# Splitting the queries and keys of an attention step into high and low fp32r parts, scores as three passes

## What is computed

```python
qa = rms_norm(heads(qa, N_HEADS_A), g_qa)      # 8 heads of 64, the same for ka, qb, kb
...
def forget_attend(q, k, v, Fq, Fk, qpos, kpos):
    logits = jnp.einsum('bthd,bshd->bhts', q, k).astype(jnp.float32) * (HEAD_DIM ** -0.5)
    logits = logits + (jnp.transpose(Fq, (0, 2, 1))[:, :, :, None] - jnp.transpose(Fk, (0, 2, 1))[:, :, None, :])
    logits = jnp.where((kpos[None, :] <= qpos[:, None])[None, None], logits, MASK_VALUE)
    p = jax.nn.softmax(logits, axis=-1).astype(v.dtype)
    return jnp.einsum('bhts,bshd->bthd', p, v)
```

## Time and profile before

| | us |
|---|---|
| median of three runs | 978.58 (977.5 to 979.12) |
| the profiled execution | 978.89 |
| its span | 977.1 |
| TensorE busy | 940.6 (96% of the span) |
| VectorE busy | 489.6 (50%) |
| ScalarE busy | 393.0 (40%) |
| GpSimd busy | 139.6 (14%) |
| mean granted TensorE clock | 0.982 of full |

### The profile page before, as it was taken

How to read it: one execution, slowest core, us unless ns; L and a number is a source line. 1 busy time by engine, 2 the same in 40 slices (tenths; PEclk the granted TensorE clock), 3 DMA queues, 4 the chain that set the end, 5 groups by cost and what they waited for, 6 DMA issues and landing times.

```text
span 977.1 us, 19815 instructions
## 1 busy us (share of the span) xinstructions
PE 940.6 (96%) x7546; PEld 861.4 (88%) x7546; DVE 489.6 (50%) x1154; ACT 393.0 (40%) x813; POOL 139.6 (14%) x139
## 2 busy tenths in 40 slices
PE   8889989899999989999999998999999999999998
PEld 7588668778788878998899998999999999999997
DVE  2553767864635686841157547454333244542232
ACT  3254655654566766433223224433211134431221
POOL 4100232141234575300000000000000000000000
PEclk9789999999999999999899999999999999999999
DMA  9536673354423564777323330323322333223212
GB/s 317 199 104 181 183 256 115 114 163 128 140 71 92 170 211 144 237 218 238 107 65 91 105 87 23 109 86 94 100 86 86 90 101 89 86 87 104 89 44 88
DMA packets 176233, 124.54 MB, mean 127 GB/s; under 512 B 14739, under 2 KB 152019, under 8 KB 176164
## 3 DMA queue, kind: packets, MB, share of 16 engines
q1 hardware_dynamic: 176034, 123.50, 41.5%
q10 hardware_dynamic: 130, 0.10, 0.0%
HBM read 116.99 MB, written 6.59 MB: 126 GB/s over the span
## 4 chain that ended last, share of the span: by engine, by line
PE 71%; issue 19%; DVE 7%; ACT 2%; POOL 1%; POOLq 0%; ACTq 0%; DVEq 0%
PE bank L952 19%; PE bank L953 18%; PE bank L954 18%; PE bank L1033 2%; PE bank L1056 2%; PE bank L1012 2%; PE bank L1042 2%; PE bank L859 1%; PE bank L1074 1%; PE bank L881 1%; PE bank L1087 1%; PE bank L1018 1%; PE bank L1097 1%; DVE sel L1881 1%; DVE ms L1926 0%
## 5 line engine op out<-in xcount | busy, mean ns | idle before, releaser
L952 PE MATMUL bank<-h_hi,w_hi 128*128 128x260 f32 x1360 | 397.3, 292 | 9.8 <-DVE h_lo L1765 6.5
L953 PE MATMUL bank<-h_lo,w_hi 128*128 128x260 f32 x1360 | 388.1, 285 | 0.0
L954 PE MATMUL bank<-h_hi,w_lo 128*128 128x260 f32 x1360 | 387.7, 285 | 0.0
L952 PEld LDWEIGHTS bank<-h_hi,w_hi 128*128 128x128 f32 x1360 | 259.8, 191 | 32.5 <-issue 24.4
L953 PEld LDWEIGHTS bank<-h_lo,w_hi 128*128 128x128 f32 x1360 | 260.1, 191 | 0.0
L954 PEld LDWEIGHTS bank<-h_hi,w_lo 128*128 128x128 f32 x1360 | 259.9, 191 | 0.0
L952 PE MATMUL bank<-u_hi,w_hi 128*128 128x260 f32 x512 | 145.2, 284 | 0.0
L953 PE MATMUL bank<-u_lo,w_hi 128*128 128x260 f32 x512 | 144.8, 283 | 0.0
L954 PE MATMUL bank<-u_hi,w_lo 128*128 128x260 f32 x512 | 144.8, 283 | 0.0
L2222 DVE TENSOR_TENSOR w_lo<-raw,w_hi 128x1024 fp32r<-128x1024 f32 x62 | 76.0, 1226 | 135.1 <-ACT w_hi L1641 135.1
L1641 ACT ACTIVATE w_hi<-raw 128x1024 fp32r<-128x1024 f32 x62 | 65.4, 1055 | 140.3 <-PE bank L954 140.3
(11 more groups left out here) (316 smaller groups left out, 1178.1 us busy)
## 6 DMA issues: line engine op xcount, KB each, us to landing
raw<-in_w_in SPq DMA_DIRECT2D x44, 512.0 KB, 4.1
part<-in_w_ada SPq DMA_DIRECT2D x32, 512.0 KB, 5.6
raw<-in_w_up SPq DMA_DIRECT2D x32, 512.0 KB, 4.1
raw<-in_w_down SPq DMA_DIRECT2D x32, 512.0 KB, 4.1
ada<-in_w_ada SPq DMA_DIRECT2D x4, 2048.0 KB, 13.6
kv<-in_cache_k_b SPq DMA_DIRECT2D x16, 256.0 KB, 4.3
qbc<-q_d SPq DMA_DIRECT2D x16, 256.0 KB, 5.0
kv<-in_cache_k_a SPq DMA_DIRECT2D x16, 256.0 KB, 4.3
```

The source lines that it names most:

```text
L952: mm(out, hi[:, k, :], x_h, start=first and k == ks[0], stop=False)
L953: mm(out, hi[:, k, :], x_l, start=False, stop=False)
L954: end = mm(out, lo[:, k, :], x_h, start=False, stop=last and k == ks[-1])
```

## The change

Two more tiles, `q_lo` and `k_lo`; `q_fm` and `k_fm` become `q_hi` and `k_hi`, of type fp32r, written by the same two ScalarE copies. A new VectorE function, `rest_back`, subtracts the high part from what stands in bank 3 and increments a new semaphore, `back_split`. It is called in step 4 for the queries, behind `rest_o` and ahead of `top_round`, and in step 7 for the keys, behind `logits` and ahead of `top_round`. All of TensorE's waits on `back_read` become waits on `back_split` of the same value. The scores of a unit pair are six fp32r matmuls in three passes in place of two fp32 matmuls. The scratch for dynamic DMAs is set to 1024 bytes.

```diff
@@ -181,6 +181,8 @@
         sm_tok_s = new("sm_tok_s", [NS, P])
         page_row = new("page_row", [1, NS * NPAGE], I32)
 
+        q_lo = new("q_lo", [P, 2, SEQ], F32R)
+        k_lo = new("k_lo", [P, 2, SEQ], F32R)
         x_t = new("x_t", [P, NCH, T])
         raw = new("raw", [P, RAW, NCH, P])
         w_hi = new("w_hi", [P, SPL, NCH, P], F32R)
@@ -197,10 +199,10 @@
         sq = new("sq", [P, SEQ])
         tok = new("tok", [P, 2, SEQ])
         z = new("z", [P, 3, SEQ])
-        q_fm = new("q_fm", [P, 2, SEQ])
+        q_hi = new("q_hi", [P, 2, SEQ], F32R)
         pad_at = place["at"]
         place["at"] += 4096
-        k_fm = new("k_fm", [P, 2, SEQ])
+        k_hi = new("k_hi", [P, 2, SEQ], F32R)
         v_tok = new("v_tok", [P, 2, QB, P])
         ki2 = new("ki2", [P, SEQ])
         lgs = sb("lgs", [P, NPAGE, 2, NS * H], F32, place["at"] - 1536)[0]
@@ -373,6 +375,7 @@
         v_ready = sem("v_ready")
         back_done = sem("back_done")
         back_read = sem("back_read")
+        back_split = sem("back_split")
         s_done = sem("s_done")
         lg_ready = sem("lg_ready")
         e_ready = sem("e_ready")
@@ -1001,7 +1004,7 @@
                     pe.wait_ge(cond_kept, 1)
                 elif h % 2 == 0:
                     pe.wait_ge(mod_ready, ADA_BLOCKS + h // 2)
-                    pe.wait_ge(back_read, 2 * p)
+                    pe.wait_ge(back_split, 2 * p)
                     before = sum(at[0] < p for at in SIDE)
                     if before:
                         pe.wait_ge(side_read, before)
@@ -1027,11 +1030,14 @@
                 if U >= 2:
                     pe.wait_ge(lg_ready, U)
                 if U % 8 == 0:
-                    pe.wait_ge(back_read, 2 * p + 2)
-                for hh in range(2):
-                    rows = slice(64 * hh, 64 * hh + 64)
-                    mm(bank[4 + hh][:, 0:width(qb)], q_fm[rows, p % 2, qb * P:(qb + 1) * P],
-                       k_fm[rows, p % 2, 0:width(qb)], start=True, stop=True).then_inc(s_done, 1)
+                    pe.wait_ge(back_split, 2 * p + 2)
+                for n, (q_part, k_part) in enumerate(((q_hi, k_hi), (q_hi, k_lo), (q_lo, k_hi))):
+                    for hh in range(2):
+                        rows = slice(64 * hh, 64 * hh + 64)
+                        last = mm(bank[4 + hh][:, 0:width(qb)], q_part[rows, p % 2, qb * P:(qb + 1) * P],
+                                  k_part[rows, p % 2, 0:width(qb)], start=n == 0, stop=n == 2)
+                        if n == 2:
+                            last.then_inc(s_done, 1)
 
             def turn_probs(U):
                 qb = unit(U)[2]
@@ -1080,7 +1086,7 @@
                 if p == 0 and kd == 0:
                     pe.wait_ge(smt_ready, 1)
                 if 2 * p + kd >= 1:
-                    pe.wait_ge(back_read, 2 * p + kd)
+                    pe.wait_ge(back_split, 2 * p + kd)
                 if kd == 0:
                     pe.wait_ge(mod_ready, ADA_BLOCKS + sum(at[0] <= p for at in ADA_AT) // 2)
                 for t in range(QB):
@@ -1478,9 +1484,9 @@
                 if kd == 0:
                     if p >= 2:
                         act.wait_ge(s_done, 8 * (p - 1))
-                    A(q_fm[:, p % 2, :], bank[3][:, :], ACT.Copy, scale=gq[:, col:col + 1]).then_inc(back_read, 1)
+                    A(q_hi[:, p % 2, :], bank[3][:, :], ACT.Copy, scale=gq[:, col:col + 1]).then_inc(back_read, 1)
                 else:
-                    A(k_fm[:, p % 2, :], bank[3][:, :], ACT.Copy).then_inc(back_read, 1)
+                    A(k_hi[:, p % 2, :], bank[3][:, :], ACT.Copy).then_inc(back_read, 1)
 
             def store_v(p):
                 act.wait_ge(tok_done, 3 * p + 3)
@@ -1944,6 +1950,20 @@
                 dve.wait_ge(back_done, 2 * p + 2)
                 dve.tensor_tensor(out, out, gk_row[:, m, :].unsqueeze(1).to_broadcast([P, 8, HD]), ALU.mult).then_inc(tok_ready, 1)
 
+            def rest_back(p, kd):
+
+                m, c = pair_mixer(p)
+                col = 1 + c if m else 0
+                dve.wait_ge(back_read, 2 * p + kd + 1)
+                if kd == 0:
+                    if p >= 2:
+                        dve.wait_ge(s_done, 8 * (p - 1))
+                    ins = dve.scalar_tensor_tensor(out=q_lo[:, p % 2, :], in0=bank[3][:, :], scalar=gq[:, col:col + 1],
+                                                   in1=q_hi[:, p % 2, :].bitcast(F32), op0=ALU.mult, op1=ALU.subtract)
+                else:
+                    ins = dve.tensor_tensor(k_lo[:, p % 2, :], bank[3][:, :], k_hi[:, p % 2, :].bitcast(F32), ALU.subtract)
+                ins.then_inc(back_split, 1)
+
             def rest_o(p):
                 dve.wait_ge(o_hi_ready, p + 1)
                 dve.tensor_tensor(o_lo[:, p, 0:SEQ], bank[7][:, :], o_hi[:, p, 0:SEQ].bitcast(F32), ALU.subtract).then_inc(o_lo_ready, 1)
@@ -2084,6 +2104,10 @@
                         normalize(p, s // 2 - 1)
                 if s == 4 and p >= 2:
                     rest_o(p - 2)
+                if s == 4 and p < N_PAIRS:
+                    rest_back(p, 0)
+                if s == K_BACK + 1 and p < N_PAIRS:
+                    rest_back(p, 1)
                 if 0 <= U < 2 * TOPK_P // 8:
                     top_round(U)
                 if s == K_BACK and p < N_PAIRS:
@@ -2276,7 +2300,7 @@
     from concourse import mybir as _mybir
     from concourse.bass_utils import run_bass_kernel_spmd as _run
 
-    nc = _bacc.Bacc("TRN2", target_bir_lowering=False, num_devices=1)
+    nc = _bacc.Bacc("TRN2", target_bir_lowering=False, num_devices=1, dynamic_dma_scratch_size=1024)
     arrays, aps = {}, {}
     for name, value in inputs.items():
         v = _np.ascontiguousarray(value)
```

## The result

The changed kernel takes 990.73 us (median of four runs, 989.9 to 993.09) against 978.04 for the kernel before in the same comparison: ratio 1.0137, 95% interval 1.0111 to 1.0163, so 12.7 us slower by the medians (the ratio is taken over the runs and is not the quotient of the two medians). Run again on a second chip it was 991.81 against 976.73, ratio 1.0157 (1.0132 to 1.0182), 15.1 us. The forecast was 994.0, range 983 to 1003. The profiled execution took 989.9 us, with a span of 988.1.

What follows compares the result with a forecast made beforehand. The prediction took TensorE, busy 96% of the span, and its waits to bound the kernel. Its terms, -2.5 + 5.1 + 10.1 - 0.6 + 3.0 = +15.1 us, put 978.9 at 994.0 us, range 983 to 1003.

Steps and rivals of the forecast that it cites:

- Term 1: Score matmuls on TensorE: three fp32r passes shorten wide groups and lengthen the narrowest, -2.5 us.
- Term 2: Query subtraction in step 4: VectorE reaches normalize later, so TensorE's key transposes wait longer, +5.1 us.
- Term 3: Key subtraction in step 7: five odd side steps on bank 3 now wait for VectorE, +10.1 us.
- Term 4: VectorE catches up while TensorE stands in step 7, so the wait behind its masks goes, -0.6 us.
- Term 5: TensorE's clock: longer standstills bring two more half-rate stretches at some 1.5 us, +3 us.
- the narrow matmul at plain fp32's pace: Rival on the score matmuls: 128-column fp32r passes run at 1.67 ns a column, 996.8 us; chance 0.13.
- the heads one after another: Rival on the score matmuls: fp32r doesn't run two heads side by side, 1005 us; chance 0.07.
- repaid: Rival: VectorE starts next steps early, halving the two subtractions' costs, with no further slow stretch, 983.4 us; chance 0.16.
- Every long standstill is followed by a slow stretch: Rival on TensorE's clock: all five long standstills bring half-rate stretches, costing 8.5 us, 999.5 us; chance 0.17.
- Faster: Rival: the subtractions lie in VectorE's idle time, leaving only the score matmuls' saving, 976.4 us; chance 0.07.

Runs made afterwards that it cites:

- no_rest: Changed kernel without both subtractions, all three passes reading only the high parts: 972.93 us, ratio 0.9979 to the kernel before.
- no_query_rest: Changed kernel without the query subtraction, the third pass reading q_hi again: 985.72 us, ratio 1.0099 to the kernel before.
- no_key_rest: Changed kernel without the key subtraction, the second pass reading k_hi again: 978.87 us, ratio 1.0025 to the kernel before.
- sides_bank2: Changed kernel with all side steps of pairs 1 to 6 in bank 2, both subtractions kept: 980.4 us, ratio 1.0035 to the kernel before.
- layout: Kernel before with the two added tiles, unused, and the smaller DMA scratch: 976.3 us, ratio 0.9995 to the kernel before.
- filled: Changed kernel with 77 useless matmuls in TensorE's standstills of steps 6 and 7: 987.43 us, ratio 1.0122 to the kernel before.
- recut2: Changed kernel with keys in bank 2, side steps in bank 3, query subtraction behind normalize, key subtraction first in step 7, earlier side-step copies: 977.65 us, ratio 0.9995.

## Why the prediction was right

It held: sign, range, and the sum within 2.4 us of the first comparison (15.1 forecast, 12.7 measured) and on the point in the second (15.1). The waits are as forecast; that the sum fits so closely is in part luck, as the terms show:

- **Term 1**, -2.5 from -2.0 and -3.3. The groups went from 0.42, 0.63, 0.85 and 1.06 us to 0.48, 0.55, 0.73 and 0.89: -0.31 a pair, -2.5 in all, and `no_rest` gave 2.4 (its interval 0.2 to 4.0). The narrow group did become longer, by 0.06 where 0.08 was forecast; that its weights bound it was argued from the earlier trace rows and not tested.
- **Term 2**, +5.1: the wait grew by 4.6, and `no_query_rest` took exactly that away. Pair 1's, where the subtraction waits for the query copy, is the longest at 3.24 us, up 1.3 as worked out. The 0.4 us of pairs 5 and 6 did not come: the six waits are those of the other pairs. Shown.
- **Term 3**, +10.1: 9.7 in five waits, the longest 2.9 where "over 3" was forecast. Shown by `no_key_rest` and `sides_bank2`.
- **Term 4**, -0.6: the wait behind the masks fell by 0.4. `layout` has 1.4 us there with the instructions of the kernel before, so this size varies between executions.
- **Term 5**, +3.0: the number of stretches was wrong. The pair stage has six slow stretches where there were two, so four more, not two: a second one on end of the first in pair 1, and one each behind the standstills of 2.9 us in pair 2, 2.4 in pair 4 and 2.0 in pair 7, the last of which was not on the prediction's list. At the 1.2 us of `filled`'s profile that is +4.8, where 2 x 1.5 was forecast; at the 0.3 or 0.7 us of its ratios it would be 1.2 or 2.7, so the price stays open.

**When the clock falls** the runs do not settle. Length alone does not decide: no slow stretch follows the 2.3 us in pair 2 or the 2.6 in pair 1 of the changed kernel, nor the 3.2 us in pair 1 of `sides_bank2`, while the kernel before has one behind 1.9 us. In pair 1 of the changed kernel the clock falls 1.3 us before the standstill ends. Filling the standstills took five of six stretches away, so they do bring them about. The Trainium skill's rule (TensorE: Matmul & The Clock Gate, "Why this matters for your kernels"), that idle gaps between bursts send the engine back to half rate, agrees with the four new stretches and with `filled`, and not with the 3.2 us of `sides_bank2`; there the measurement decides. The page speaks of long gaps only, so the prediction read more into it than it says when it had every one of the five bring a slow stretch.

Sum of the measured terms, with term 5 at 4.8: -2.5 + 4.6 + 9.7 - 0.4 + 4.8 = 16.2; the wait for `o_lo` adds 0.4. The pair stage grew by 16.4 against the profile of the kernel before and by 15.4 against `layout`. Term 5 came out 1.8 larger than forecast by this price, terms 2 and 3 together 0.9 smaller. That the first comparison shows 2.4 us less than the second is within their intervals.

Of the rivals, the narrow matmul at plain fp32's pace and the heads one after another fall by the score rows; "repaid" falls too, since no half of terms 2 and 3 went. "Every long standstill is followed by a slow stretch" falls by the two that have none. "Faster" falls by the added waits of 2.4 to 2.9 us. `no_rest` shows term 1 alone left only where the subtractions are not made at all; with both made and off TensorE's path, `recut2` reached 0.9995 (0.9975 to 1.0014) and did not show it.

What stays open: where `recut2`'s 2.3 us behind L1469 come from, whether it is faster than the kernel before at all, and what besides a standstill makes the clock fall.

## What to carry to other kernels

Here a saving on the busiest engine was paid for on the engine that must prepare its operands, and the price is not that engine's added time (8 x 0.75 and 8 x 0.68, 11.4 us in 16 instructions, in an engine half idle) but where in its queue the new instruction stands and who now waits for it. When one semaphore is replaced by a later one everywhere, look at each wait separately: here one harmless-looking reuse of a bank cost 11 of 15 us, and another bank took it away. Standstills of 2 to 3 us can cost more than their length, since the clock fell behind four of them here, though not behind all.

## What the hardware showed that was not expected

- Work that computes nothing raised the granted clock: with 77 matmuls (128 columns, plain fp32) put into TensorE's standstills and every useful instruction still there, the pair stage's clock was 0.99 in place of 0.96 and the profiled stage 6.0 us shorter than 285.6. By the ratios of the whole kernel the gain was 1.5 or 3.4 us, which is not clear of the noise.
- Three fp32r passes with 64 rows each run two heads side by side as plain fp32 does: 0.89 us for 3 x 2 x 512 columns. An estimate of 3 x 0.21 = 0.64 for the columns, one per cycle of 2.4 GHz, leaves 0.25 us around them, and this fits the four widths within 0.02 us, except the narrowest (0.48 against 0.41). There the passes start 0.16 and 0.12 us apart, near the 0.115 us at which 128-column weights followed one another in the earlier trace rows.
- GpSimd's power of only 8 columns takes 1.64 us, and in pair 5 it sets the pace of `normalize` once VectorE is early.
